# Spreading decay rows over the partitions: GpSimd's broadcast in place of 40 one-hot matmuls

## The reference, cut to what matters

```python
# mamba2_ssd: 16 heads, two chunks of 128 tokens
log_decay = jnp.cumsum(dt * a, axis=2)
seg = log_decay[:, :, :, None] - log_decay[:, :, None, :]
decay = jnp.exp(jnp.where(causal, seg, -jnp.inf))
y = jnp.einsum('bclsg,bclsge,bcsgep->bclgep', cb, decay, x_dt)
# mlstm_chunkwise: 4 heads
d = cum_f[:, :, :, None] - cum_f[:, :, None, :] + log_i[:, :, None, :]
m_row = jnp.maximum(jnp.max(d, axis=3), inter)
w_intra = jnp.exp(d - m_row[:, :, :, None])
```

## Time and profile before

| what | before |
|---|---|
| median of 3 runs | 441.48 us |
| lowest and highest run | 441.07, 442.28 us |
| span of the profiled execution, first to last instruction | 440.2 us |
| PE busy | 420.8 us, 96% |
| DVE busy | 278.1 us, 63% |
| ACT busy | 247.3 us, 56% |
| POOL busy | 31.9 us, 7% |

### The profile page before, as it was taken

How to read it: one execution, slowest core, us unless ns; L and a number is a source line. 1 busy time by engine, 2 the same in 40 slices (tenths; PEclk the granted TensorE clock), 3 DMA queues, 4 the chain that set the end, 5 groups by cost and what they waited for, 6 DMA issues and landing times.

```text
span 440.2 us, 6837 instructions
## 1 busy us (share of the span) xinstructions
PE 420.8 (96%) x2716; PEld 378.8 (86%) x2716; DVE 278.1 (63%) x384; ACT 247.3 (56%) x325; POOL 31.9 (7%) x24
## 2 busy tenths in 40 slices
PE   3799999999999999989999699999999999999996
PEld 3699999878888888767888699999999999999995
DVE  2769849947564688778744755655655655656553
ACT  6568887583466764988434545544544544444430
POOL 2004426401010000000000000000000000000000
PEclk9999999999999999999999699999999999999999
DMA  7775455653534323325546085656655655566202
GB/s 200 237 251 165 132 184 190 194 191 113 174 98 149 136 98 104 127 103 204 170 153 192 0 269 163 208 160 191 188 177 181 190 186 191 191 191 191 95 1 95
DMA packets 45485, 70.80 MB, mean 161 GB/s; under 512 B 4926, under 2 KB 27670, under 8 KB 45462
## 3 DMA queue, kind: packets, MB, share of 16 engines
q1 hardware_dynamic: 45462, 70.48, 49.4%
HBM read 69.42 MB, written 1.05 MB: 160 GB/s over the span
## 4 chain that ended last, share of the span: by engine, by line
PE 91%; ACT 4%; DVE 2%; DMA 2%; issue 1%; SPq 0%; DVEq 0%
PE pj L1088 23%; PE pj L1090 23%; PE pj L1089 23%; PE mx L1134 6%; PE mx L1088 4%; PE mx L1089 4%; PE mx L1090 4%; PE mx L1131 2%; DMA wraw<-in_w_in 2%; ACT whi L383 1%; ACT L519 1%; DVE wlo L705 1%; ACT sz_b L519 0%; DVE acc L1043 0%; ACT seg_b L526 0%
## 5 line engine op out<-in xcount | busy, mean ns | idle before, releaser
L705 DVE TENSOR_TENSOR wlo<-wraw,whi 128x2048 fp32r<-128x2048 f32 x60 | 137.4, 2291 | 106.0 <-ACT whi L383 105.9
L383 ACT CAST whi<-wraw 128x2048 fp32r<-128x2048 f32 x65 | 123.9, 1908 | 110.4 <-PE pj L1090 80.1
L1088 PE MATMUL pj<-hT_hi,whi 128*128 128x256 f32 x512 | 147.1, 287 | 3.3 <-DVE hT_lo L724 3.3
L1089 PE MATMUL pj<-hT_lo,whi 128*128 128x256 f32 x512 | 146.5, 286 | 0.0
L1090 PE MATMUL pj<-hT_hi,wlo 128*128 128x256 f32 x512 | 146.5, 286 | 0.0
L1088 PEld LDWEIGHTS pj<-hT_hi,whi 128*128 128x128 f32 x512 | 100.1, 195 | 4.5 <-DVE wlo L705 3.4
L1089 PEld LDWEIGHTS pj<-hT_lo,whi 128*128 128x128 f32 x512 | 100.1, 196 | 0.3
L1090 PEld LDWEIGHTS pj<-hT_hi,wlo 128*128 128x128 f32 x512 | 99.9, 195 | 0.0
L1088 PE MATMUL pj<-whi,hT_hi 128*128 128x512 f32 x144 | 57.7, 401 | 0.0
L1090 PE MATMUL pj<-whi,hT_lo 128*128 128x512 f32 x144 | 56.2, 390 | 0.0
L1089 PE MATMUL pj<-wlo,hT_hi 128*128 128x512 f32 x144 | 56.1, 390 | 0.0
(11 more groups left out here) (202 smaller groups left out, 440.8 us busy)
## 6 DMA issues: line engine op xcount, KB each, us to landing
wraw<-in_w_in SPq DMA_DIRECT2D x24, 1024.0 KB, 5.2
wraw<-in_ffn_w_up SPq DMA_DIRECT2D x44, 512.0 KB, 4.7
wraw<-in_ffn_w_down SPq DMA_DIRECT2D x11, 1024.0 KB, 4.8
wraw<-in_w_out SPq DMA_DIRECT2D x8, 1024.0 KB, 4.8
x_sb<-in_x SPq DMA_DIRECT2D x2, 512.0 KB, 4.0
out_x<-x_sb SPq DMA_DIRECT2D x1, 512.0 KB, 2.7
out_x<-x_sb SPq DMA_DIRECT2D x2, 256.0 KB, 2.0
seg_b<-in_w_in SPq DMA_DIRECT2D x1, 64.0 KB
```

Of the source, the lines that this page charges most:

```text
L383: nc.scalar.copy(whi[:, slot, :], wraw[:, slot, :]).then_inc(s.hi_done, 1)
L705: nc.vector.tensor_tensor(wlo[:, slot, :], wraw[:, slot, :], whi[:, slot, :].bitcast(F32), ALU.subtract).then_inc(s.lo_done, 1)
L1088: pe_mm(ps, a_hi, b_hi, start=start, stop=False, skip_group_check=shared)
L1089: pe_mm(ps, a_hi, b_lo, start=False, stop=False, skip_group_check=shared)
```

## The change

The one-hot matmuls are gone, and with them the hi and lo parts of `ld` and `mrow`. ACT issues five small DMAs that lay the rows of four heads end to end in one partition (`mflat` in `st_b`, `ldrow` in `so_b`, one partition for each j), and POOL's `partition_broadcast` writes such a row of 1024 values to all partitions, straight into the tile where the exponential is to stand. ACT's exponentials then read and write that tile in place. A `seg` half is spread again (j = 2, 3) only when `y_out` has read it and its mask is done. PE's `xs_turn` and `qk_turn` wait for other semaphores, since they no longer share PSUM with the spread rows.

```diff
@@ gpsimd
-            for u in POOL_UNITS:
-                if u < 10:
-                    split(u)
+            def spread_ld(j):
+                if j >= 2:
+                    pool.wait_ge(s.y_ps, j - 1)
+                    pool.wait_ge(s.seg_masked, j)
+                pool.partition_broadcast(seg_b[:, (j % 2) * 1024:(j % 2 + 1) * 1024],
+                                         ldrow[32 * j:32 * j + 1, :]).then_inc(s.ldb_spread, 1)
+                pool.wait_ge(s.ldb_spread, j + 1)
+
+            split(4)
+            pool.wait_ge(s.m_flat, 16)
+            pool.wait_ge(s.lo_pool, 1)
+            pool.partition_broadcast(Wm_b[:, 0:1024], mflat[0:1, :]).then_inc(s.mb_spread, 1)
+            pool.wait_ge(s.mb_spread, 1)
+            split(6)
+            split(8)
...
+            pool.wait_ge(s.w_sel, 1)
+            pool.wait_ge(s.ld_flat, 16 * 4)
+            spread_ld(0)
+            spread_ld(1)
             for u in POOL_UNITS:
                 if 10 <= u < 13:
                     split(u)
             for j in range(4):
+                if j >= 2:
+                    spread_ld(j)
                 pool.wait_ge(s.seg_exp, 4 * NT * (j + 1))
@@ scalar
-                act.wait_ge(s.mb_ps, 1)
+                act.wait_ge(s.mb_spread, 1)
...
-                        nc.scalar.activation(Wm[:, h, c, :], mb[:, h, c, :], ACT.Exp, scale=-1.0,
+                        nc.scalar.activation(Wm[:, h, c, :], Wm[:, h, c, :], ACT.Exp, scale=-1.0,
...
-            def rows_split():
+            def rows_flat():
 
                 act.wait_ge(s.rows_mx, 1)
-                nc.scalar.copy(ld_hi[:, :], ld[:, :]).then_inc(s.rows_hi, 1)
-                nc.scalar.copy(mrow_hi[:, :], mrow[:, :]).then_inc(s.rows_hi, 1)
+                act.dma_start(mflat[0:1, :].rearrange("o (h t) -> o h t", h=4), mrow[:, :]).then_inc(s.m_flat, 16)
+                for j in range(4):
+                    act.dma_start(ldrow[32 * j:32 * j + 1, :].rearrange("o (h t) -> o h t", h=4), ld[4 * j:4 * j + 4, :]).then_inc(s.ld_flat, 16)
...
-            at(3, rows_split)
+            first_at(3, rows_flat)
...
-            nc.scalar.copy(one_hot[:, :], ident[0:16, 0:16]).then_inc(s.one_hot_ready, 1)
@@ tensor
-            at(4, m_rows_out)
...
-                at(10 + 2 * j, ld_out, j)
...
-                pe.wait_ge(s.w_exp, MH * NT)
+                pe.wait_ge(s.cols_ready, 3)
...
-                pe.wait_ge(s.seg_exp, 4 * NT * (3 + i))
+                pe.wait_ge(*((s.bc_copied, 2), (s.qk_normed, 1))[i])
```

More of the change, by code:

```diff
@@ L94, in build @@
         ones = sb("ones", [16, P])
-        one_hot = sb("one_hot", [16, 16], F32R)
         bias3 = sb("bias3", [P, 4])
@@ L99, in build @@
         ld = sb("ld", [16, T])
[L100 to L103, removed]
         mrow = sb("mrow", [4, T])
@@ L118, in build @@
         seg_b = sb("seg_b", [P, 2048])
-        seg = seg_b[:, :].rearrange("p (a c h l) -> p a c h l", a=2, c=NT, h=4)
+        seg = seg_b[:, :].rearrange("p (a h c l) -> p a c h l", a=2, c=NT, h=4)
         prow1, prow2 = seg_b[:, 0:P], seg_b[0:4 * FC + 2, P:2 * P]
@@ L142, in build @@
         st_b = sb("st_b", [P, 1024])
+        ldrow, mflat = so_b, st_b
         Sst = st_b[:, :].rearrange("p (g n) -> p g n", g=NG)
@@ L172, in build @@
             par_T par_cols ssq1 ms1 rt1 xn_rows hT_ps hi_T lo_T w24_hi w24_lo small_ps
-            rows_abs rows_e rows_v rows_l expa_r rows_mx rows_ex rows_sc cols_ps cols_ready
-            mb_ps w_exp w_sel vec conv_base conv_done conv_act mv_ready mo_ready av_ready z_ready
+            rows_abs rows_e rows_v rows_l expa_r rows_mx m_flat ld_flat mb_spread ldb_spread rows_ex rows_sc cols_ps cols_ready
+            w_exp w_sel vec conv_base conv_done conv_act mv_ready mo_ready av_ready z_ready
             xs_ps xs_done bc_ps bc_copied st_ps st_copied inter_ps inter_done
-            one_hot_ready ldb_ps seg_exp seg_masked mt_ready y_ps y_added
+            seg_exp seg_masked mt_ready y_ps y_added
             kt_ps ktok_ready sc_ps sw_ready cst_ps cst_copied num0_ps nu_part int1_ps int1_done num1_ps
-            h_ready mnorm_sq mnorm_ssq mnorm_rt ml_rows mlT_ps mlT_hi mlT_lo rows_hi rows_lo
+            h_ready mnorm_sq mnorm_ssq mnorm_rt ml_rows mlT_ps mlT_hi mlT_lo
             qk_sq qk_ms qk_rt qk_rows qkT_ps qk_normed s_ps p_masked p_exp p_scaled pT_ps pT_copied o_ps att_hi att_lo
@@ L446, in w_exp @@
             def w_exp():
-                act.wait_ge(s.mb_ps, 1)
+                act.wait_ge(s.mb_spread, 1)
                 act.wait_ge(s.cols_ready, 3)
-                mb = mx[1][:, :].rearrange("p (h c t) -> p h c t", h=MH, c=NT)
                 for h in range(MH):
                     for c in range(NT):
-                        nc.scalar.activation(Wm[:, h, c, :], mb[:, h, c, :], ACT.Exp, scale=-1.0,
+                        nc.scalar.activation(Wm[:, h, c, :], Wm[:, h, c, :], ACT.Exp, scale=-1.0,
                                              bias=cols[:, C_G[c] + h:C_G[c] + h + 1]).then_inc(s.w_exp, 1)
@@ L465, in seg_exp @@
             def seg_exp(j):
-                act.wait_ge(s.ldb_ps, j + 1)
-                if j >= 2:
-                    act.wait_ge(s.y_ps, j - 1)
+                act.wait_ge(s.ldb_spread, j + 1)
                 for c in range(NT):
                     for h in range(4):
-                        nc.scalar.activation(seg[:, j % 2, c, h, :], mx[0][:, h * T + c * P:h * T + (c + 1) * P], ACT.Exp,
+                        nc.scalar.activation(seg[:, j % 2, c, h, :], seg[:, j % 2, c, h, :], ACT.Exp,
                                              bias=cols[:, C_LD[c] + 4 * j + h:C_LD[c] + 4 * j + h + 1]).then_inc(s.seg_exp, 1)
@@ L772, in rows_dec @@
                 nc.vector.tensor_tensor(r_dec[:, 0:P], r_dec[:, 0:P], r_u[:, 0, 0:P], ALU.mult).then_inc(s.rows_sc, 1)
[L774 to L778, removed]
             def cols_copy():
@@ L1217, in inter @@
                 ins.then_inc(s.inter_ps, 1)
[L1219 to L1231, removed]
             def y_out(j):
```

## The result

| what | before | after |
|---|---|---|
| median of 4 runs, on one chip | 441.88 us | 463.31 us |
| lowest and highest run | 441.07, 443.26 | 463.07, 464.02 |
| ratio, with its 95% interval | | 1.0484 (1.0463 to 1.0504) |
| span of the profiled execution | 440.2 | 462.0 |
| PE busy | 420.8 | 420.3 |

What follows compares the result with a forecast made beforehand. PE was taken to bound the kernel, busy 420.8 of 440.2 us. Unit 10's lateness +15.0, clock +1.6 and four blocks -4.5 gave +12.1, a span of 452.3; with 1.3 for the median, 453.6 us, range 443 to 461.

Steps and rivals of the forecast that it cites:

- the first switch: At the start of POOL's list: the one switch the kernel before already has costs at most 0.23 us.
- Start: Start of the kernel: taken as 0, with 1.28 us as upper bound for ACT's later table load.
- Unit 10's lateness: PE's start of unit 10: 15.0 us late, twice a POOL switch of 7.5, the removed 1.03 contained.
- Clock: PE after the wait at unit 10: a low granted clock loses 1.6 us, added once.
- The blocks: On PE's chain: the four removed `ld` matmul blocks of 1.12 us each save 4.5 us.
- behind unit 10 nothing is late: After unit 10: split 12 comes in time and the third `seg` broadcast's switch is hidden, so no loss.
- the larger of 6.3 and two switches: At unit 10: ACT's delay (6.3 us on PE) and POOL's two switches run side by side, giving 15 us.
- rival A: The forecast: both switches ahead of unit 10 cost, together 10 to 19 us, giving 448.6 to 457.6; chance 0.52.
- C: At unit 10: the switch back is free (0.23), both together 7.7 us; +3.2, 444.7 us; chance 0.11.
- D: Switches cost next to nothing, so only ACT's wait is left: +1.8, 443.3 us; chance 0.10.
- E: Not slower: ACT's wait is cheaper (5.2 us late) and switches are free; +0.1, 441.6 us; chance 0.05.
- Rival B: Dear POOL switches of 10.4 us each, as weight loads and code share DMA engines; 460.2 us; chance 0.18.

Runs made afterwards that it cites:

- e1: The kernel before, with one broadcast of 128 values that nobody reads added at the very end of POOL's list: 447.53 us.
- e3: The kernel before, with one unread broadcast of 128 values between POOL's mask of `Wm` and its split of unit 10: 448.84 us.
- e9: The changed kernel, with one tiny two-input subtraction that nobody reads added at the very end of POOL's list: 458.59 us.
- e4: The changed kernel, with ACT's five DMA issues moved back behind the row exponentials: 457.09 us.
- e2: The kernel before, with ACT's two small casts, which wait for the rows' maxima, moved ahead of the cast of unit 5: 449.46 us.
- e8: The changed kernel, with the rows spread by DMAs over a DRAM scratch from POOL's queue, without POOL's broadcasts and ACT's DMA issues: 440.06 us.
- e12: The changed kernel, with all splits on DVE, ACT's five DMA issues behind the row exponentials, and a tiny subtraction last in POOL's list: 452.34 us.
- e11: The changed kernel, with ACT's five DMA issues behind the row exponentials and a tiny subtraction last in POOL's list: 452.27 us.
- e10: e8 with ACT's copies `cst_copy` and `nu0_copy` put ahead of `seg_exp`: 439.18 us.

## Why the prediction was wrong

**The step that failed** is the one on the first switch: "The only one that before has costs at most the 0.23 us ahead of its neighbour; but it stands at the start, where nothing was changed yet." I read the start as untouched because its instructions were. By e1, e3 and e9, which take the cost to the start and away from it, the row was cheap because POOL's list ended on the splits' code; with a list that ends on the broadcast's code it isn't. It took 9.85 us, and PE's unit 4 ended 5.2 late. In the profile of before the only hint was that a row of the same kind as the five new ones stood there; the question "what does it find when the kernel runs again?" was not asked.

**The sum, term by term.** Predicted +12.1, measured +21.8 in the spans:

- Start: 0 predicted, 5.2 measured. The 1.28 us table load that I bounded there was hidden (ACT waited for `ident` behind it).
- Unit 10's lateness: 15.0 predicted. Without the start it is 21.6 - 5.2 = 16.4. The term that was mis-sized is ACT's DMA issues: 1.20 + 4 x 0.60 = 3.7 us, not 1.7 from SP's row; they shift the mask of `Wm`, from which POOL's two switches count. The switches themselves were right: 7.24 and 7.16 for 7.5, and the two broadcasts 2.70 for 2.2. The mask at 81.07 + 1.11, then 7.24 + 2.70 + 7.16 + 4.51, gives 103.8.
- Clock: 1.6 predicted from the earlier trace rows, 2.9 measured in unit 10. That a loss behind unit 4 is absorbed held: unit 10 waits for POOL whatever units 5 to 9 do.
- The blocks: -4.5 predicted. They went, but 1.7 came back at `y_out(1)` and `y_out(2)`, where PE is now early and ACT's chain isn't shorter. The prediction said "behind unit 10 nothing is late"; that was wrong by this term.

12.1 + 5.2 + 1.4 + 1.3 + 1.7 = 21.7, against 21.8.

**Half right:** "the larger of 6.3 and two switches ... and not their sum". It gave the right number for this kernel, but not because ACT's delay costs nothing. Split 10 had 6.88 us of idle time ahead of it, and ACT's delay, predicted at 6.9 and 8.4 at the mask of `Wm` (81.07 for 67.48, less the start's 5.2), had used them up before the switches came. e4 takes the delay away: the mask of `Wm` starts at 72.8 and not 81.1, unit 10 at 96.5 and not 103.9, and 6.2 us are gained. e2 has the delay alone and costs 7.4, by its wait and the clock behind it.

**Right, and shown:** POOL's switches, PE's wait for them and ACT's wait, each in its place and within 1.3 us. The third `seg` broadcast's switch (7.44) was hidden. So rival A described the middle of the kernel; rivals C, D and E fell with the measured switch of some 7 us in each direction. Rival B came near the time for a reason that did not hold: no switch between units took 10.4.

The Trainium skill (GPSIMD Engine Reference, Instruction dispatch) gives 5.95 us for the first call after a load, with no instruction in the profile. The rows agree in kind, and show more: 6.9 to 8.5 us in the middle (5.9 once, at the end of e1), 9.2 to 10.8 at the start.

## What to carry to other kernels

Count a code switch of GpSimd, some 7 us here, for each change of kind in its list, and treat the list as a ring: in these 14 kernels the code on which it ended set what its first mask cost. Before trading engine time for a transport, price the transport where it is waited for; here 5.5 us of matmuls were given for switches of 7 us each in an engine whose splits had 7 us of slack, and a plain DMA over DRAM did the same without a switch, though its landing has to be watched (ACT waited 1.92 us for it in e8). And a gain on the critical engine only arrives as far as the next engine's chain is early: ask at each place behind the edit who now comes last.

## What the hardware showed that was not expected

**POOL's instructions and a DVE pass with two inputs in SBUF exclude each other.** In the kernel after, the last broadcast takes 3.26 us instead of 1.30:

```profile
149.63 3.26 POOL L350 PARTITION_BROADCAST seg_b<-so_b  x1 [2.99 <-PE mx L1137]
```
```profile
149.43 2.29 DVE L715 TENSOR_TENSOR wlo<-wraw,whi 128x2048 fp32r<-128x2048 f32 x1 [0.96 <-ACT whi L396]
```

DVE began first and ended at 151.7; 1.30 more is 153.0, and the broadcast ends at 152.9. In e12 it is the other way round: the broadcast runs first, from 48.53 for 1.30, and DVE's small product, begun 0.02 us later, ends with it and takes 1.28 instead of 0.27, which is PE's wait of 1.1 there:

```profile
48.55 1.28 DVE L777 TENSOR_TENSOR sz_b<-sz_b,xdt_b 16x128 f32<-16x128 f32 x1
```

It is not the broadcast alone. POOL's split of unit 6 in e4, begun 0.43 us behind DVE's subtraction, takes 6.21 and not 4.61, and PE was waiting for it:

```profile
60.37 6.21 POOL L343 TENSOR_TENSOR wlo<-wraw,whi 128x2048 fp32r<-128x2048 f32 x1 [7.27 <-issue]
```
```profile
59.94 2.28 DVE L715 TENSOR_TENSOR wlo<-wraw,whi 128x2048 fp32r<-128x2048 f32 x1
```

In e11 the same split takes 6.57 us. Beside DVE's `conv_taps`, of whose tiles one is in PSUM, the splits keep their 4.6.

The Trainium skill (SBUF — State Buffer, SBUF: two separate sides) has this as an exclusive lock on a port pair that the two engines share, taken for the whole instruction; these rows agree. No run was made to tell it apart from another cause.

**The low clock does not last equally long.** After a wait of 4.3 us PE was back at 1.00 only 9 us later (e2), after 8.3 us 5.7 later (unit 10 of the kernel after), after 2.1 some 4.6 later (e8), and after 1.1 in e10 the windows behind show 1.00. Nor does the length of the wait say whether the clock falls: behind 1.6 us at `y_out(2)` it stayed at 1.00 (the kernel after and e8), behind 1.3 us in e10 it was 0.50. What ends it was not tried.

**Issuing a DMA is not one price.** On ACT the row of `mrow` took 1.20 us and each `ld` row 0.60; on POOL 0.5 to 0.7; on SP 0.32.
